# Attention projection stage: the query/key normalisation moved ahead of other VectorE work in each unit, the modulation sums moved to the end

## What is computed

```python
mod = silu(c) @ ada_w[i] + ada_b[i]                 # 6 * 1024 columns per layer
sh1, sc1, g1, sh2, sc2, g2 = split(mod, 6)
h = rms_norm(x, norm_mix[i]) * (1.0 + sc1) + sh1
qkv = h @ w_qkv                                      # 3 groups x (q, k, v) x 1024 columns
for g, (window, dil) in enumerate(((128, 1), (512, 4), (2048, 16))):
    q = rms_norm(qkv[:, :, g, 0], q_gain[g])         # per head, over 128
    k = rms_norm(qkv[:, :, g, 1], k_gain[g])
    o, m, l = banded causal softmax attention of q, k, v with a relative bias
merge the three groups by their softmax denominators; y = merged @ w_out
x = x + g1 * y
```

## Time and profile before

| | |
|---|---|
| median of 3 runs | 863.06 us |
| the profiled execution | 863.67 us |
| its span, first to last instruction | 861.9 us |
| TensorE busy | 835.1 us (97%) |
| VectorE busy | 611.7 us (71%) |
| ScalarE busy | 432.4 us (50%) |
| GpSimd busy | 123.7 us (14%) |
| mean granted TensorE clock | 0.994 of 2.4 GHz |

### The profile page before, as it was taken

One profiled execution on the slowest core, in us unless ns is written; L12 is line 12 of the kernel. 1 busy time (PEld: TensorE's weight loads), 2 busy tenths in 40 slices (PEclk: granted clock), 3 DMA queues, 4 the chain that ended last, 5 costly groups with the idle time before them and its releaser, 6 DMA issues.

```text
span 861.9 us, 10974 instructions
## 1 busy us (share of the span) xinstructions
PE 835.1 (97%) x4254; PEld 697.2 (81%) x4254; DVE 611.7 (71%) x749; ACT 432.4 (50%) x549; POOL 123.7 (14%) x154
## 2 busy tenths in 40 slices
PE   4999999999999999999999999999999999999998
PEld 2778888878878987888888887888888788887886
DVE  4897798787888776577566685787867756644544
ACT  5365464454535666443344366778575635434431
POOL 3000101111110100011010000467810000000000
PEclk9899999999999999999999999999999999999999
DMA  9997888886977835688788755434254567765521
GB/s 320 366 357 249 284 275 269 281 256 219 281 260 241 263 115 189 190 277 294 253 278 267 248 169 173 147 103 143 98 179 129 182 220 244 243 201 170 191 97 50
DMA packets 122103, 188.98 MB, mean 219 GB/s; under 512 B 5683, under 2 KB 91048, under 8 KB 122052
## 3 DMA queue, kind: packets, MB, share of 16 engines
q1 hardware_dynamic: 109796, 146.10, 52.3%
q0 software_dynamic: 12256, 42.18, 14.6%
HBM read 187.18 MB, written 1.09 MB: 218 GB/s over the span
## 4 chain that ended last, share of the span: by engine, by line
PE 81%; DVE 9%; ACT 5%; issue 3%; DMA 1%; POOL 1%; SPq 0%; DVEq 0%; ACTq 0%; POOLq 0%
PE bank L516 66%; PE bank L632 2%; PE bank L738 2%; PE bank L712 2%; ACT whi L980 2%; DVE wlo L1355 2%; DVE acc L1376 1%; PE bank L907 1%; PE bank L585 1%; PE bank L851 1%; PE bank L693 1%; DMA x<-in_x_dram 1%; PE bank L582 1%; PE bank L721 1%; DVE wlo L1363 1%
## 5 line engine op out<-in xcount | busy, mean ns | idle before, releaser
L1355 DVE TENSOR_TENSOR wlo<-raw,whi 128x2048 fp32r<-128x2048 f32 x120 | 278.5, 2326 | 41.1 <-ACT whi L980 41.0
L980 ACT ACTIVATE whi<-raw 128x2048 fp32r<-128x2048 f32 (+1 forms) x124 | 235.6, 1901 | 22.8 <-DMA raw<-in_attn_w_qkv_dram 13.3
L516 PE MATMUL bank<-whi,hT_hi 128*128 128x512 f32 (+1 forms) x728 | 195.5, 392 | 0.9 <-DVE arena L1593 0.9
L516 PE MATMUL bank<-wlo,hT_hi 128*128 128x512 f32 (+1 forms) x752 | 195.0, 382 | 1.3 <-DVE wlo L1363 1.3
L516 PE MATMUL bank<-whi,hT_lo 128*128 128x512 f32 (+1 forms) x728 | 187.5, 380 | 0.0
L516 PEld LDWEIGHTS bank<-wlo,hT_hi 128*128 128x128 f32 x752 | 138.0, 189 | 30.3 <-DVE wlo L1363 2.5
L516 PEld LDWEIGHTS bank<-whi,hT_lo 128*128 128x128 f32 x728 | 133.2, 188 | 26.5
L516 PEld LDWEIGHTS bank<-whi,hT_hi 128*128 128x128 f32 x728 | 130.0, 189 | 27.4 <-issue 3.4
L393 POOL DMA_DIRECT2D ada_w<-in_ada_w_dram x80 | 42.6, 533 | 513.6 <-DVE acc L1376 496.4
L1376 DVE SCALAR_TENSOR_TENSOR acc<-ada_w,cact,acc 128x1024 f32<-128x1024 f32 x80 | 102.3, 1279 | 7.4 <-DMA ada_w<-in_ada_w_dram 5.1
L1216 ACT ACTIVATE arena<-bank 128x256 f32<-128x256 f32 x44 | 14.5, 381 | 166.9 <-PE bank L516 166.9
(11 more groups left out here) (185 smaller groups left out, 839.5 us busy)
## 6 DMA issues: line engine op xcount, KB each, us to landing
raw<-in_ffn_w_dram SPq DMA_DIRECT2D x88, 512.0 KB, 4.9
ada_w<-in_ada_w_dram POOLq DMA_DIRECT2D x80, 512.0 KB, 4.9
raw<-in_attn_w_qkv_dram SPq DMA_DIRECT2D x62, 512.0 KB, 6.4
raw<-in_ffn_w_dram SPq DMA_DIRECT2D x22, 1024.0 KB, 5.0
raw<-in_hgrn_w_in_dram SPq DMA_DIRECT2D x16, 1024.0 KB, 5.6
arena<-in_ada_w_dram SPq DMA_DIRECT2D x16, 512.0 KB, 10.3
raw<-in_attn_w_qkv_dram SPq DMA_DIRECT2D x4, 1024.0 KB, 7.6
raw<-in_attn_w_out_dram SPq DMA_DIRECT2D x4, 1024.0 KB, 6.7
```

Source lines behind the costliest of these rows:

```text
L516: mm = nc.tensor.matmul(dst[t][c][:, 0:n], lhs[:, k0 + k, t * P:(t + 1) * P], w[:, k, c * 512:c * 512 + n], start=start and k == 0, stop=s ...
L980: return nc.scalar.activation(dst, src, ACT.Copy)
L1355: nc.vector.tensor_tensor(wlo[:, m % RAW, :], raw[:, m % RAW, :], fp(hi_of(m)), ALU.subtract).then_inc(s["split"], 1)
```

## The change

In the attention projection VectorE does three things in another order, and ScalarE one.

- In pairs 1 to 3, `qk_normalise` follows directly on `att_max`, then come `att_normalise` and, last, the `ada_op`s.
- In the first pair (units 3 to 8), `qk_normalise` of the chunk before stands ahead of `split_unit(m + 2)`.
- In the first pair `qk_rsqrt` on ScalarE stands ahead of `round_unit(m + 2)`.

```diff
 ScalarE
             def qkv_extra(m):
                 pr, j = divmod(m, QU)
-                if qk_last(m - 1) is not None:
+                if pr and qk_last(m - 1) is not None:
                     qk_rsqrt(qk_last(m - 1))
...
             for m in range(2, PURE):
+                if m < QU and qk_last(m - 1) is not None:
+                    qk_rsqrt(qk_last(m - 1))
                 round_unit(m + AHEAD)
                 qkv_extra(m)
...
 VectorE
                 if pr >= 1 and j % 2 == 0 and j < 8:
                     att_max(J)
+                if pr and qk_last(m - 1) is not None:
+                    qk_normalise(qk_last(m - 1))
+                if pr >= 1 and j % 2 == 0 and j < 8:
+                    att_normalise(J)
                 for n in range(ada_done(m - 1), ada_done(m)):
                     ada_op(n)
-                if pr >= 1 and j % 2 == 0 and j < 8:
-                    att_normalise(J)
-                if qk_last(m - 1) is not None:
-                    qk_normalise(qk_last(m - 1))
                 if qk_last(m) is not None:
                     qk_reduce(qk_last(m))
 
             for m in range(2, PURE):
+                if m < QU and qk_last(m - 1) is not None:
+                    qk_normalise(qk_last(m - 1))
                 split_unit(m + AHEAD)
                 qkv_extra(m)
```

## The result

| | before | changed |
|---|---|---|
| median | 863.68 us (862.61 to 865.84, 4 runs) | 872.71 us (870.69 to 874.35, 4 runs) |
| ratio, with its 95% interval | | 1.0113 (1.0092 to 1.0134) |
| span of the profiled execution | 861.9 us | 872.6 us |

The forecast was 861.7 us with 857.0 to 867.0 as its range, so it was wrong, and on the other side of "no change". Rival B, the ring as the bound, is what happened, and it cost more than B's 868.9 us. The profiled execution of the changed kernel is the longest of its four (874.35 us), so its trace shows 10.7 us more than before where the medians differ by 9.0.

The account below looks back on a forecast made before the run. TensorE was taken as the bound, busy 835.1 of 861.9 us. From 863.67 us, 5.3 won and 3.9 of new waits gave 862.3, and the median's 0.6 us below the profiled execution made it 861.7; range 857.0 to 867.0 us.

Parts of the forecast that it names:

- Rival B: Sums in the units between: VectorE waits for ada_w in every one, copies out of bank 7 late; 868.9 us, chance 0.14.
- What bounds the kernel: TensorE, busy 835.1 of 861.9 us; only its waits, 5.4 us of them aimed at, or its lower clock can be won.
- What the change wins: Five waits at the query/key transposes go, 4.5 us, and unit 6's wait shrinks by 0.8: 5.3 us won.
- The first pair's later rounding and splitting, costed at nothing: Units 3 to 8: they come 1 to 3.5 us later, wanted 7 us and more after being made; no cost.
- What it costs: Sums moved behind the exponential return the two ada_w slots later; with loads landing in 5.0 us, new waits 3.9 us.
- rival A: The ada_w ring keeps up: loads land in about 4.1 us, 0.4 us of new waits; 856.7 us, chance 0.19.
- The four places: New TensorE waits at unit 11, 0.85 us; unit 12, 1.2; unit 14, 1.1; units 30 to 32, 0.7.
- Tasks "costed at nothing": Tasks after units 19, 23, 27 and 28 have 1 to 5 us of slack and are costed at nothing.
- Clock: Slow stretch from 195.4 to 200, say 1.5 us, goes; unit 32's new wait may bring another; the two cancel.
- Rival C: New waits lower the clock: three slow stretches of 1.5 us instead of one; 864.7 us, chance 0.07.
- Wrong: waits at 738 in pairs 2 and 3 as well (then B): Sign against the forecast: TensorE waits at line 738, for the task copy, also in pairs 2 and 3.

Follow-up runs that it names:

- e3: The kernel before with only the first pair's part of the change; 862.88 us, ratio 0.9993.
- e9: The changed kernel with the second gate row as a third ada_w slot for loads 16 to 47; 865.52 us, ratio 1.0029.
- e13: e9 with the order of the kernel before from VectorE's unit 27 on, where two slots are left; 857.92 us, ratio 0.9950.
- e4: The changed kernel with modulation loads 18 to 63 halved, its modulation wrong, run for time alone; 867.03 us, ratio 1.0048.
- e7: The changed kernel with SyncE's weight loads of units 14 to 39 issued 3 to 4 us later; 881.52 us, ratio 1.0219.
- e10: The changed kernel, two slots, with a unit's first sum ahead of output and maximum and the other behind them; 861.02 us, ratio 0.9978.
- e11: The changed kernel with e9's third slot, first sum ahead of output and maximum, the other between normalisation and division; 858.21 us, ratio 0.9956.
- e2: The changed kernel without the first pair's part, on ScalarE and VectorE; 871.03 us, ratio 1.0096.

## Why the prediction was wrong

- **What bounds the kernel**, and **What the change wins**: right. All five waits at line 693 went, the collision with the clearing went with them, and unit 6's wait went to nothing. 5.4 us were won, 5.3 had been said.
- **The first pair's later rounding and splitting, costed at nothing**: right; e3 alone is at 0.9993.
- **The step that failed is in "What it costs": the landing, taken as 5.0 us "since the trace's median is over the same mix of traffic".** It was not the same mix. The change moves the refills by 2 us and more, to where a weight slot comes free, and they landed in 5.8 us in the median. The new waits came to 12.1 us where 3.9 had been said. What set each was one refill: 7.2 us ahead of unit 11's wait, 5.8 ahead of unit 14's, 7.5 and 7.1 ahead of the one at 582, 7.8 ahead of the last. Ahead of unit 12's it was 4.9, and there the forecast held. I had written down this very thing as an argument in rival A (the later issue meets SyncE's) and did not draw it into the sum. At 5.8 us my own working gave 868.9. That the two slots, and not the order by itself, made such landings cost time is what e9 shows: with a third slot the loads took as long, and the first five waits went.
- **The four places.** Forecast and measured, in us: unit 11, 0.85 and 2.23; unit 12, 1.2 and 0.94; unit 14, 1.1 and 1.62; units 30 to 32, 0.7 and 3.51. The places and lines were right, and three of the four sizes too small. The last was "sized by the first", although SyncE's loads there are a megabyte with the bias rows behind them, and it met a landing of 7.8 us. A median landing can't price a wait that one long landing sets.
- **Tasks "costed at nothing", with 1 to 5 us of slack**: 2.07 us at task 5 (line 582) and 0.42 at line 738 in pair 2, and 1.25 behind the projection. That cover was indeed the first to go, as the sentence said; no price stood beside it.
- **Clock, "I let the two cancel"**: the second step that failed, wrong by 3.3 us. With the waits' 8.2 us it makes up the distance from the forecast's - 1.4 us to the + 10.0 of the books. The stretch removed was worth 1.6 us, the new one 4.9. I sized the new one by the old, whose wait was 0.5 us; e13 measures it as 4.7 us. Rival C had the mechanism and gave 1.5 us to each.
- **Rivals and chances**: B had 0.14 and was the case. What had to be seen is that the sign hung on one number: slower from 5.3 us on (a straight line between its own values at 5.0 and 5.8 gives 5.2), with the trace's own at 5.0 and a reason at hand for it to rise. With 0.2 to 0.3 us between the value taken and the change of sign, B should have had about the chance of the forecast.
- **"Wrong: waits at 738 in pairs 2 and 3 as well (then B)"**: only one of 0.42 us came at 738 in pair 2, none in pair 3; the loss there surfaced at 582 and 721 instead.

## What to carry to other kernels

A prefetch ring of few slots is timed by the distance from giving a slot back to its next use. When consumers of the ring are moved behind a long step, work out that distance for each unit and set it against a long landing, not the median, taken anew for the moment when the refill will go out. Everything in program order behind a consumer that waits is late with it. A reordering that loses may be right in itself: here the same order lost 1.1% with two slots and, with a third one in memory that lay idle for most of the stage and the old order for the last units, won 0.5%.

## What the runs showed that I had not expected

- A load's landing hung on what had been issued ahead of it about as much as on its size. The refills of 512 KB in the changed kernel took 6.4 us in the mean within 3 us behind a SyncE load and 5.3 us otherwise; those of 256 KB (e4) took 5.5 and 3.7 us, and one of them 8.4 us, behind 1 MB and the bias rows. This is read from the traces; no run has held everything else fixed.
- The clock answered to short waits where small matmuls followed, and not in proportion to them. From the transposes ahead of the late sixteen one-column matmuls to the next scores takes 8.35 us at full speed. It took 4.9 us more behind 3.51 us of wait (the changed kernel), 4.7 behind 3.62 (e9), 3.3 behind 4.13 (e4), 1.7 behind 2.60 (e7), 3.3 behind 1.08 (e10) and 0.1 behind 0.85 (e11). In the kernel before, 0.51 us ahead of the earlier sixteen lost 1.6 us, and 1.67 us at 249 us, with full units behind it, nothing (the first product of the next took 1.18 us). What decides the size is not shown. In the changed kernel the wait of 3.5 us so became one of 8.4 us.
- Executions of one kernel differ by the same thing: of the twelve of e10, the four with a mean granted clock of 0.995 or 0.996 took 857.1 to 859.1 us, the eight with 0.990 to 0.992 took 860.7 to 864.1. The trace shown is one of the eight.
- Five raw slots instead of six cost 11 us, and in the trace all of it behind 298 us: 6 us of waits for `hT_hi`, and the rest at other places. I have not looked into why.

What stays open: the share of the 5.0 to 5.8 us that is due to SyncE's loads alone, and how e2 came to have other waits than the changed kernel for nearly the same time.
